# Split-weight stream for the mixer projections, with branch results parked in memory

## The reference

```python
xn = rms_norm(x, norm_mix)
(r_q, r_k, r_v, r_g, h_q, h_f, h_i, h_g, g_qkv, g_g, g_a, g_b, d_q, d_k, d_v, gate_in) = jnp.split(
    xn @ w_in, ...)
# four branches, 4 heads of 128: retention, HGRN2, gated DeltaNet, differential attention
branches = jnp.stack([o_ret, o_hgrn, o_gdn, o_diff], axis=2)
gates = jax.nn.sigmoid(gate_in.reshape(b, t, N_BRANCH, D_MODEL))
merged = jnp.einsum('btnc,ncd->btnd', branches, w_branch)
h = x + jnp.sum(gates * merged, axis=2) @ w_out
y = h + peer_ffn(rms_norm(h, norm_ffn), ...)
```

## Time and profile before

| | |
|---|---|
| time, median of 3 runs | 5701.8 us (5701.15 to 5711.91) |
| the profiled execution | 5703.9 us, span 5702.2 us |
| PE busy, share of the span | 5397.2 us, 95% |
| PE weight loads | 4850.2 us, 85% |
| DVE busy | 3392.3 us, 59% |
| ACT busy | 1849.1 us, 32% |
| POOL busy | 624.6 us, 11% |
| granted TensorE clock, mean | 0.970 |

### The profile page before, as it was taken

The page is one execution under the profiler, slowest core; times in us unless marked ns, Lnnn a source line. Parts: engine busy times, 40 slices in busy tenths (PEclk is TensorE's granted clock), DMA queues, the critical chain, the costliest instruction groups (busy, mean ns, idle before and its releaser), DMA issues. The chain is left out here.

```text
span 5702.2 us, 84468 instructions
## 1 busy us (share of the span) xinstructions
PE 5397.2 (95%) x31154; PEld 4850.2 (85%) x31154; DVE 3392.3 (59%) x6723; ACT 1849.1 (32%) x2766; POOL 624.6 (11%) x518
## 2 busy tenths in 40 slices
PE   8999997999998999999989999979999989999998
PEld 6777876998998999999867778759989989999998
DVE  3443544434899775677634535444348997757775
ACT  2322222323322553333223222222233235533332
POOL 0000000000222111222100000000002221112221
PEclk9999997999999999999999999979999999999999
DMA  3222221222777898888632212212237779988886
GB/s 115 64 63 62 54 75 35 93 81 109 234 250 238 275 287 319 322 309 308 237 107 70 61 58 58 81 29 89 83 108 243 253 230 282 288 318 321 304 315 231
DMA packets 498388, 1006.05 MB, mean 176 GB/s; under 512 B 85620, under 2 KB 306804, under 8 KB 496244
## 3 DMA queue, kind: packets, MB, share of 16 engines
q1 hardware_dynamic: 424356, 733.55, 39.1%
q0 software_dynamic: 73728, 268.47, 13.5%
HBM read 851.08 MB, written 153.16 MB: 176 GB/s over the span
## 5 line engine op out<-in xcount | busy, mean ns | idle before, releaser
L1675 PE MATMUL ps<-parts,splits 128*128 128x448 f32 (+1 forms) x7488 | 1464.0, 355 | 3.4 <-DVE ix L2165 3.4
L1675 PEld LDWEIGHTS ps<-parts,splits 128*128 128x128 f32 x7488 | 1326.8, 188 | 92.5 <-issue 4.1
L2296 PE MATMUL ps<-parts,splits 128*128 128x448 f32 x6144 | 1245.9, 365 | 4.3 <-DVEq L2344 4.3
L2296 PEld LDWEIGHTS ps<-parts,splits 128*128 128x128 f32 x6144 | 1153.8, 188 | 96.4 <-DVEq L2344 5.1
L166 PE MATMUL ps<-xn,wr 128*128 128x288 f32 x1952 | 495.8, 409 | 13.1 <-PEq L106 10.7
L166 PEld LDWEIGHTS ps<-xn,wr 128*128 128x128 f32 x1952 | 364.0, 190 | 126.3 <-issue 33.7
L2021 DVE TENSOR_TENSOR splits<-raw,splits 128x1024 fp32r<-128x1024 f32 x288 | 352.9, 1225 | 149.0 <-ACT splits L1913 144.7
L1431 PE MATMUL ps<-parts,wmh 128*128 128x288 f32 x2048 | 413.7, 298 | 28.0 <-DVE parts L1489 28.0
L1431 PEld LDWEIGHTS ps<-parts,wmh 128*128 128x128 f32 x2048 | 330.3, 189 | 29.6 <-issue 29.6
L1708 POOL IOTA iota<- 128x128 f32 x2 | 0.5, 228 | 2803.7 <-POOLq L106 2803.7
L1913 ACT CAST splits<-raw 128x1024 fp32r<-128x1024 f32 x288 | 304.7, 1058 | 8.4 <-DVE second L2016 4.8
(11 more groups left out here) (411 smaller groups left out, 8210.6 us busy)
## 6 DMA issues: line engine op xcount, KB each, us to landing
raw<-in_u SPq DMA_DIRECT2D x256, 512.0 KB, 5.1
raw<-in_v SPq DMA_DIRECT2D x128, 512.0 KB, 11.5
more<-in_v SPq DMA_DIRECT2D x128, 512.0 KB, 12.1
activated<-go SPq DMA_DIRECT2D x256, 224.0 KB, 1.9
coefficients<-wt SPq DMA_DIRECT2D x28, 2048.0 KB, 9.4
wr<-in_w_cm SPq DMA_DIRECT2D x104, 512.0 KB, 4.3
first<-activated SPq DMA_DIRECT2D x32, 896.0 KB, 6.6
wb<-coefficients SPq DMA_DIRECT2D x32, 896.0 KB, 9.1
```

The costliest lines, as they stand in the source:

```text
L1675: last = nc.tensor.matmul(out, wp[:, slot, k, :], xp[:, k, cols], start=(k == 0 and wp is T.wh and xp is T.xh), stop=(k == KD - 1 and wp i ...
L2296: last = nc.tensor.matmul(out, vp[:, r % 4, m * P:(m + 1) * P], coef, start=(r == 0 and vp is T.vh and gp is T.xh), stop=(ends and vp is T ...
```

## The change

The weights come as one stream, in the order of use, of 15 tiles a head, the value columns among them. Each tile is loaded into one of two raw slots, rounded by ACT into one of three slots of `T.ih`, and its remainder is put into `T.il` by DVE. The semaphores of the stream live through the layer. A load waits for the DVE subtraction of the tile two before it.

```diff
+STREAM_ENTRY = 5
+STREAM_HEAD = 15
+WSLOTS = 3
+def stream_tile(n):
+    order = (3, 4, 5, 6, 7, 8, 9, 10, 11, 12, 0, 1, 2, 13, 14)
+    h, i = divmod(n + STREAM_HEAD - STREAM_ENTRY, STREAM_HEAD)
+    return h - (i < 10), order[i]
...
+def load_weight(sp, T, l, n):
...
+    if n >= 2:
+        sp.wait_ge(T.flow["w_low"], n - 1)
+    sp.dma_start(T.iraw[:, n % 2], T.d["w_cm"][l, h, column]).then_inc(T.flow["w_raw" + str(n % 2)], 16)
+def act_weight_high(nc, act, T, n):
+    act.wait_ge(T.flow["w_raw" + str(n % 2)], 16 * (n // 2) + 16)
+    nc.scalar.copy(T.ih[:, weight_slot(n)], T.iraw[:, n % 2]).then_inc(T.flow["w_high"], 1)
+def dve_weight_low(nc, dve, T, n):
+    slot = weight_slot(n)
+    dve.wait_ge(T.flow["w_high"], n + 1)
+    nc.vector.tensor_tensor(T.il[:, slot], T.iraw[:, n % 2], T.ih[:, slot].bitcast(F32), ALU.subtract
+                            ).then_inc(T.flow["w_low"], 1)
+def projection(nc, T, out, n, a, first=0, count=KD):
+    slot, cols = weight_slot(n), slice(a * HALF, (a + 1) * HALF)
+    for k in range(first, first + count):
+        for wp, xp in ((T.ih, T.mh), (T.ih, T.ml), (T.il, T.mh)):
+            last = nc.tensor.matmul(out, wp[:, slot, k, :], xp[:, k, cols], start=(k == 0 and wp is T.ih and xp is T.mh),
+                                    stop=(k == KD - 1 and wp is T.il))
+    return last
+def token_projection(nc, T, out, t, weights):
+    for k in range(KD):
+        for wp, xp in ((T.ih, T.mh), (T.ih, T.ml), (T.il, T.mh)):
+            last = nc.tensor.matmul(out, tile(xp[:, k, :], t), weights(wp, k),
...
 def pe_ahead(nc, pe, T, s, start, u, b, banks=1, first=0, count=KD):
...
-        if a == 0 and loads:
-            pe.wait_ge(s["w"][slot], 16 * loads)
+        if a == 0:
+            pe.wait_ge(T.flow["w_low"], n + 1)
...
-    for k in range(first, first + count):
-        last = nc.tensor.matmul(bank(T, b)[:, 0:HALF], T.wr[:, slot, k, :], T.xn[:, k, a * HALF:(a + 1) * HALF],
-                                start=(k == 0), stop=(k == KD - 1))
+    last = projection(nc, T, bank(T, b)[:, 0:HALF], n, a, first, count)
...
+def store_branch(sp, T, b, h):
+    c = branch_number(b, h)
+    sp.wait_ge(T.flow["br_done"], c + 1)
+    sp.dma_start(T.d["branches"][4 * b + h], T.bo[:, c % 2, :]).then_inc(T.flow["br_out" + str(c % 2)], 16)
```

The input is kept as `T.mh` and `T.ml`. In the entry stage DVE scales a row in place and, two rows behind, subtracts what ACT has rounded:

```diff
+            scale(0)
+            scale(1)
+            for k in range(KD):
+                if k + 2 < KD:
+                    scale(k + 2)
+                dve.wait_ge(s["x_high"], k + 1)
+                nc.vector.tensor_tensor(T.ml[:, k, 0:N], T.h[:, k, :], T.mh[:, k, 0:N].bitcast(F32), ALU.subtract
+                                        ).then_inc(s["x_low"], 1)
+            for n in range(1, STREAM_ENTRY):
+                dve_weight_low(nc, dve, T, n)
```

```diff
-            if more:
-                value_tile(0)
             for c in range(2):
                 pe.wait_ge(s["sq_done"], c + 1)
                 wide_product(nc, T, 4 + 2 * c, lambda kk: T.general[:, C_COMP:C_COMP + P], lambda kk: sq[c],
                              1).then_inc(s["ss_done"], 1)
             if more:
+                value_tile(0)
                 value_tile(1)
...
             if more:
+                copy_values(0)
                 copy_values(1)
+                act_weight_high(nc, act, T, start + 15)
...
+            if more:
+                dve_weight_low(nc, dve, T, start + 15)
             diagonals(0)
```

`dve_finish` writes to one of two rows of `T.bo`; the next stage begins with `store_branch`, which writes it to memory. `merge_stage` reads the branches back, four rows at a time, into the memory that holds `T.mt`, and uses `T.mh` and `T.ml` as its split input:

```diff
+            sp.wait_ge(s["br_out0"], 128)
+            load_branches(0)
             sp.dma_start(T.wm[1], T.d["w_merge"][l, 0, 1]).then_inc(w_in[1], 16)
+            sp.wait_ge(s["br_out1"], 128)
+            load_branches(1)
+            for b in (2, 3):
+                sp.wait_ge(s["b_low"], 4 * b - 4)
+                load_branches(b)
...
-            for k in range(KD):
-                nc.scalar.copy(T.xh[:, k, :], T.xn[:, k, 0:N]).then_inc(s["x_high"], 1)
-                if k == 3:
-                    high(0, 0, 1)
+            high(0, 0, 1)
             for r in range(16):
-                nc.scalar.copy(T.brh[:, r, :], T.br[:, r, :]).then_inc(s["b_high"], 1)
-                if r == 11:
+                if r % 4 == 0:
+                    act.wait_ge(b_in[r // 4 % 2], 16 * (r // 8) + 16)
+                nc.scalar.copy(T.brh[:, r, :], T.bi[:, r % 8, :]).then_inc(s["b_high"], 1)
+                if r == 3:
                     high(1, 1, 1)
```

More of the change, by code:

```diff
@@ L510, in _ @@
                 nc.scalar.activation(T.rs, T.rs, ACT.Exp, scale=-0.5).then_inc(s["late_root"], 1)
+            act_weight_high(nc, act, T, start + 1)
             take(0)
             take(1)
+            act_weight_high(nc, act, T, start + 2)
+            act_weight_high(nc, act, T, start + 3)
             act_square(nc, act, T, s)
             act_root(nc, act, T, s)
-            for u in range(2, 6):
-                take(u)
+            take(2)
+            take(3)
+            act_weight_high(nc, act, T, start + 4)
+            take(4)
+            take(5)
         @block.vector
@@ L772, in ahead @@
                 c, a = divmod(u, 2)
-                wslot, loads = ATT_SLOTS[c]
+                number = start + 7 + (c if n < 4 else c)
                 if first == 0:
-                    if a == 0 and loads:
-                        pe.wait_ge(s["w"][wslot], 16 * loads)
+                    if a == 0:
+                        pe.wait_ge(T.flow["w_low"], number + 1)
                     if n == 2:
@@ L780, in ahead @@
                         pe.wait_ge(s["taken"], n)
-                for kk in range(first, first + count):
-                    last = nc.tensor.matmul(spare(n), T.wr[:, wslot, kk, :], T.xn[:, kk, a * HALF:(a + 1) * HALF],
-                                            start=(kk == 0), stop=(kk == KD - 1))
+                last = projection(nc, T, spare(n), number, a, first, count)
                 if first + count == KD:
@@ L988, in _ @@
                     nc.scalar.copy(kss[:, 0:NS], bank(T, 6)[:, 0:NS]).then_inc(s["kss_copied"], 1)
+                if more and r in (2, 4, 6):
+                    act_weight_high(nc, act, T, start + 10 + r // 2)
             for t in range(4):
@@ L1081, in _ @@
                     part(r + 1, TILES if r < 2 else 4)
+                if more and r in (2, 4, 5):
+                    dve_weight_low(nc, dve, T, start + {2: 10, 4: 11, 5: 12}[r])
                 if r == 2:
@@ L1123, in _ @@
             dve.sem_inc(s["st_ready"], 1)
+            if more:
+                dve_weight_low(nc, dve, T, start + 13)
             dve.wait_ge(s["sdelta_ready"], 1)
@@ L1331, in _ @@
             link = chained(dve, s["chain_v"])
+            if more:
+                dve_weight_low(nc, dve, T, start + 14)
             for c, dst in enumerate((q, k)):
```

320 lines of the change are left out of this document (172 added, 148 removed).

## The result

The changed kernel takes 5732.1 us (median of 6 runs, 5719.6 to 5752.7) against 5701.8 us: a ratio of 1.0055, 95% interval 1.0041 to 1.0069. A second series gave 5735.8 us and 1.0043 (1.0027 to 1.0059). The forecast was 5670 us, faster than before; the kernel is 30 us slower, inside the range of 5640 to 5745. Its runs also scatter over 33 us in the first series and 41 us in the second.

The account below looks back on a forecast made before the run. PE, busy 95% of the span, was taken as the bound. Terms -32 - 10 - 4 + 6 + 5 + 3 - 5 + 5 = -32 us gave 5670 us from the profiled 5703.9, less 2 to the median; range 5640 to 5745.

Parts of the forecast that it names:

- retention: Retention stages: six shorter units run back to back on PE and four splits fit; -4.0 us each, -32 in eight heads.
- HGRN: HGRN stages: DVE's mask and reduce steps set the pace, outputs come 1.2 us sooner; -1.3 us each, -10 in eight heads.
- GDN: GDN stages: shorter units against costlier d_v tiles; -4 us in six heads, +6 in the last heads of the two layers.
- attention: Attention stages: scores start 0.4 us sooner, but a DVE split delays the diagonals; +0.8 us each, +5 in six heads.
- entry, without its cold unit: The two entries: first unit ends 5 us later, units and value tiles give 3.5 and 3.1 back; about -1.4 each.
- merge: Start of the two merges: the first product no longer waits for the input's split; -2.7 us each, -5.
- clock, with entry's cold units: PE at 1.2 GHz: a fall in every GDN stage at 1 us, +5 taken; entry's next unit may cost 2.6 us more.
- prices on PE: Projections on PE: a unit 0.70 us less, a value tile 0.63 less, a d_v tile 0.89 more; 123 us relieved in all.
- Both rivals on narrow products: GDN's 128-column d_v tiles: four passes, 107 us more, 5777 (chance 0.08); or no load floor, 48 less, 5622 (0.08).
- Splits in the chains: Rival: six more of a head's 15 splits land on DVE's path, 59 us more, 5729; chance 0.16.
- the clock stays down: Rival: each head gets 10 us more at half clock with PE as the bound, +40, 5710; chance 0.18.
- The signal named for being wrong: Sign against the forecast, on PE: half clock in stages that had full clock; no size given.

Follow-up runs that it names:

- e_one_fill: Changed kernel plus 12 rounded products that nothing reads, in HGRN's wait for DVE's last mask: 5709.1 us, ratio 1.0003.
- e_cheap_fill: Changed kernel with 12 unread products in HGRN's last-mask wait and splits formed for one of eight slices only, from the fourth tile on: 5685.7 us.
- e_ends: Changed kernel, order only: last weight loads issued at the next stage's start, GDN's sample state products earlier, splits of tiles 13 and 15 later: 5710.9 us.

## Why the prediction was wrong

Half of PE's busy time at half clock is an estimate of what the clock costs. In HGRN it is too high: by `e_one_fill`, whose HGRN stages do not fall and take 402.8 us, the clock costs 17 us there and not 23, and the rest is -3 and not -9. Taking it out of both columns leaves what the other steps did:

| step | predicted | measured | of it clock | rest |
|---|---|---|---|---|
| retention | -32 | -29.5 | -2 | -27 |
| HGRN | -10 | +14.2 | +23 | -9 |
| GDN | +2 | +16.5 | +18 | -1 |
| attention | +5 | +24.0 | +17 | +7 |
| entry, without its cold unit | -3 | -2.8 | +7 | -10 |
| merge | -5 | -4.5 | 0 | -5 |
| clock, with entry's cold units | +10 | | | +63 |

The *prices on PE* were right. Rounded 288-column products start 0.13 us apart; the 128-column ones, which the prediction took between two bounds, 0.11 us apart at full clock:

```profile
670.61 0.27 PE L211 MATMUL ps<-il,mh 128*128 128x128 f32 x1
670.72 0.28 PE L211 MATMUL ps<-ih,mh 128*128 128x128 f32 x1
```

Both rivals on narrow products fall. *Merge* and, by the rest, *GDN* came as worked out, *retention* with 27 to 29 of its 32 us. *Splits in the chains* falls by its size, 23 us in `e_cheap_fill`, and by its sign, two waits behind `il` in the whole kernel where the prediction named more than two a head.

The step that failed is **clock**: "such a fall in every GDN stage, at 1 us ... I take +5". It looked at the one stretch where the kernel before fell and asked what would be added to it. It did not ask which stages with the full clock would lose it, though the text had what was needed: in HGRN units shorter by 0.70 us each stand ahead of chains of DVE that do not get shorter, and "DVE's mask and reduce steps set the pace". The runs show what stood there in its place: a wait of 1.93 us, and 17 us for the three stages that fall behind it. With entry's cold units the prediction had +10 for the clock; PE's time at half clock rose by 16 us a head, by the estimate +63, or +57 with HGRN as measured. The rival *the clock stays down* has the mechanism, but at 10 us a head and +40. Forecast and rival were treated as cases apart, while each microsecond of relief in front of a chain is a microsecond of waiting. The signal named for being wrong, half clock in stages that had full clock, is what the profile showed.

GDN opens a wait of the same kind, at the sum of squares behind the shortened units 0 and 1. It was 0.42 us; in the changed kernel's first GDN stage it is 1.82:

```profile
176.81 1.24 PE L142 MATMUL ps<-wk,core 128*128 128x288 f32 x4 [1.82 <-ACT pr L1033]
```

Five of the eight GDN stages have it, at 1.8 to 2.1 us, and in all five half clock of 7 or 10 us follows within 2 us. The other three are at half clock already around the stage's start. In the kernel before four of the eight have 3 us at this place and four none. So the fall in every GDN stage was forecast rightly, and its size was not: 1 us a stage against some 18 us in all by the estimate. No run fills this wait, so that it causes GDN's share is likely and not shown.

The Trainium skill (TensorE: Matmul & The Clock Gate, A second HAM failure mode: psum-queue depth-cycling) describes frequent small idle times between groups of matmuls as enough to make the gate swing between its two levels. This case agrees in kind: the swing follows a wait of 1.93 us in three of eight HGRN stages and keeps off the other five. The Trainium skill (TensorE: Matmul & The Clock Gate, Terms) prices time at half clock at one half of it; here the HGRN stage with 20 us at half clock takes 59.6 us where the same stage of the second layer, at full clock, takes 50.4: 9.2 us for 20, a little less than half.

Two smaller steps failed, and entry gained more than its -3 once the clock is taken out (-10, by the estimate; why is open). In *HGRN*, the outputs were to come 1.2 us sooner; they wait for the states, these for the masks, and came 0.2 sooner (36.9 us after the stage's start against 37.1), and the stage ends on DVE's split and SP's load: 50.4 undisturbed on average, not 49.5. In *attention* the scores were to start 0.4 us sooner; in head 2 they start 10.8 us after the stage's start against 9.1 before. PE has nothing to do until ACT's first square, 0.7 us into the stage, and then makes the sums of squares at half clock, in 3.4 in place of 1.9 us. The wait at the first turn was to grow by 0.8 us and grew by 1.8. The order cost the kernel before 18 us in these stages and gives the changed one 9 back; moving the split, in `e_ends`, gives 14. These do not add up to the 24, for each also shifts where the clock falls.

The value stage, untouched by the change, took 12 us more in the first profile, and nothing shows that the change causes it. Its products are slower evenly in some executions, as the PE groups of the second layer's value stage show, the kernel before first, then the changed one:

```profile
L2296 PE MATMUL ps<-parts,splits 128*128 128x448 f32 x3072 | 622.9, 365 | 2.2 <-DVEq L2344 2.2
```

```profile
L2414 PE MATMUL ps<-parts,splits 128*128 128x448 f32 x3072 | 635.0, 368 | 2.3 <-DVEq L2462 2.3
```

That is 0.2066 in place of 0.2027 us a product, and the stage takes 12 us longer. Of the 83 further runs of the kernel before, 54 lie between 5696 and 5705 us and 29 from 5708 up, most of these some 12 us above the first group, so it may be the same event; no profile of the kernel before caught it, and its cause is open.

## What to carry to other kernels

Before relieving an engine that runs in order, go through its waits: where another engine's chain ends at the same point, the relief becomes idle time, and on PE idle time can cost more than the relief frees. Judge such a change by the granted clock and PE's idle time of each stage, repeated over stages that run the same program, and not by one total; put moved work, or as a test products that nothing reads, into the wait that opened. Where the clock falls in some of several identical stages, an edit's time is only known by its runs.

## What the hardware showed

- Leaving out four contraction steps (eight instructions, 1.94 us) a head made the kernel before 58 us slower; adding twelve rounded products a head made the changed one 27 us faster.
- Identical stages differ by up to 9 us in one execution: the HGRN stages of the changed kernel take 49.7 to 59.6 us, and the three longest are those with 10, 10 and 20 us at half clock. Its second profile repeats them stage by stage.
- Rounded products of 128 columns run at 0.11 us, of 256 at 0.12 and of 288 at 0.13: below 288 columns almost nothing is gained, and turning the operands round took 6.6 us of PE's work out of a GDN stage.
- Products of 448 columns ran at 0.2027 or, for a whole stage of 655 us, at 0.2066 us, with the same granted clock in the profile, 0.99.
